# Decay attention: scores by three products of rounded high and low parts, and one buffer of turned shares

## The chip, the cores and the metric

The kernel runs on one core of one Trainium2 chip. The metric is the time of one execution on the device in microseconds (us). Shown times of a kernel are the median of several executions; a profiled execution has a time of its own.

## What is computed

Four layers (convolution mixer, forgetting attention, short convolution, convolution mixer) and then one more block work on a sequence of 512 tokens of width 1024 in float32. The change touches the second layer, the attention with forget gates. Cut to what matters:

```python
q = rms_norm(q.reshape(b, s_len, 16, 128), q_norm_g)
k = rms_norm(k.reshape(b, s_len, 16, 128), k_norm_g)
# per head and block of 128 queries
logits = einsum("bqhd,bkhd->bhqk", q_blk, k) * scale
logits = logits + c_blk[..., :, None] - c[..., None, :]
logits = where(causal, logits, -inf)
p = softmax(logits, axis=-1)
o = einsum("bhqk,bkhd->bqhd", p, v)
```

There are 16 heads of width 128; c is the running sum of the log forget gates. The layer's input projection makes q, k, v and a gate z; its output projection follows the attention.

## The kernel before, in words

Every engine has a program of its own, written out by hand in order, with waits on semaphores between them. Signals are counted; `wait_ge(signal, key)` waits for the step that `key` names. On an engine, everything behind a wait stands still until it is met.

Weights come in chunks of 1 MB, two slots. For each chunk ScalarE makes a rounded copy WH (`split_hi`, line 365), and the remainder WL comes about in one of two ways (`split_lo`, line 378): GpSimd subtracts, or, for chunks that `summed` names, ScalarE writes the negated rounded copy and GpSimd issues a DMA that adds the weights to it. The chunks of the attention's heads 1 to 15 are summed; the chunks of the values are not. A projection is three products in the rounded type fp32r (`gemm`): WH with HH, WH with HL, WL with HH, where HH and HL are the rounded activations and their remainder. One half of a chunk is 24 matmuls of 512 columns.

The attention (`layer_b_tensor` from line 1551, and the loops at lines 1703, 1782 and 1867 for VectorE, ScalarE and GpSimd) is a software pipeline over h from 0 to 17. In step h TensorE does, in this order: the query half of head h's projection; the turning (transposing) of the first two blocks of head h-2's shares; the key half of the projection; the other turns and, between them, the weighing of values with the shares of head h-2; the scores of head h-1 (`scores_tensor`, line 1498); the last weighing; after h = 3, 7 and 11 the values of the next four heads (96 matmuls); then the statistics of head h, the sums of squares of queries (`query_statistics_tensor`) and keys (`key_statistics_tensor`) over the 128 channels. The statistics take the rounded squares (SQHI) and their remainders (SQLO), two matmuls each, four `MR,onesr` records. In heads 0 and 1 the key's statistics stand inside the next head's projection instead, after its first six matmuls. Heads 0 and 15 (`WHOLE`) take the keys' squares whole, without a remainder.

ScalarE in step h: the split of the next chunk; the query's rounded square; two copies of turned shares (`copy_turned_scalar`, line 1751) into BPT; the key's rounded square; two more copies; the four exponentials of head h-1's softmax; then the logarithm and exponential of head h's variances, with a table load before each kind. For h = 16 it skips the first two copies, which VectorE does.

VectorE in step h: the shares of head h-2 (a reciprocal and four scalings); `normal_vector` (line 1634), which makes head h-1's normalized queries QN and keys KN by a Newton step, eight instructions; the copies of head h's raw queries and keys out of PSUM (`keep_vector`); the logits of head h-1; the output gate; the variances of head h.

GpSimd in step h: the causal fill for head h-1; `split_lo` for the next chunk; for h up to 14 the squares of queries and keys and their remainders (`square_low_gpsimd`, line 1839), four instructions; then the DMA that loads head h's decay rows. For h = 3, 7 and 11 the split is that of a value chunk, which GpSimd subtracts itself.

SyncE issues the loads of raw weights as slots come free.

BPT (line 1394) has two buffers of turned shares, taken in turn. The scores are four matmuls in fp32 on QN and KN, of 128, 256, 384 and 512 columns:

```python
pe.mm(logit_bank(h, i), QN[:, i * P:(i + 1) * P], KN[:, 0:(i + 1) * P], True, True)
```

A fp32 matmul leaves two records in the trace, a rounded one leaves one.

Of the kernel before, what the change touches and what calls it, by code (L numbers as in the profile page):

```python
# [7 lines left out]
ALU = mybir.AluOpType  # L8
ACT = mybir.ActivationFunctionType
F32 = mybir.dt.float32  # L10
F32R = mybir.dt.float32r

P = 128
# [136 lines left out]
def build_program(nc, x, vectors, b_f_bias, pe_k, w1_k, w2_k, pe_v, w1_v, w2_v, rel_bias, onehot, out,  # L150
# [3 lines left out]
    with ctx:  # L154
        def sb(name, cols, dt=F32):
            return ctx.enter_context(nc.sbuf_tensor(name, [P, cols], dt))
# [24 lines left out]
        HT = sb("HT", 2 * T)  # L181
        SQ = sb("SQ", 2 * T)
        DG = sb("DG", 2 * T)
        AR = sb("AR", 20960)
        banks = [ctx.enter_context(nc.psum_tensor(f"ps{i}", [P, T], F32)) for i in range(8)]

# [5 lines left out]

        def ar(o, n=T):
            return AR[:, o:o + n]

        def hs(tile, k, sl=slice(0, T)):
            return tile[:, k * T + sl.start:k * T + sl.stop]
# [1193 lines left out]
        b_t, b_ev, b_w, b_o, b_mask = (sig(n) for n in ("b_t", "b_ev", "b_w", "b_o", "b_mask"))  # L1391
        BZ = [ar(i * T) for i in range(KE)]
        BV = [ar(16 * T + i * NB * T, NB * T) for i in range(2)]
        BPT = [ar(24 * T + i * 1280, 1280) for i in range(2)]
        BP = [ar(29 * T + OFF[i], (i + 1) * P) for i in range(NB)]
        B1 = 29 * T + 1280
        RAW = [ar(B1 + i * T) for i in range(2)]
        QN, KN = ar(B1 + 2 * T), ar(B1 + 3 * T)
        CB, C_OFF = ar(B1 + 4 * T, 1280), [1152, 896, 512, 0]
        WHOLE = (0, 15)  # L1400
        NEGC = ar(B1 + 7 * T)
# [77 lines left out]
            op.then_inc(b_t, h, i)  # L1479

        def weigh_tensor(pe, h, i):
            s, g, o = h % 2, h // 4, (h % 4) * P
            if i == 0:
                if h % 4 == 2 and h < 12 or h == 0:
                    pe.wait_ge(b_vev_v, (h + 2) // 4, 3)
                else:
                    pe.wait_ge(b_o, h - 1)
                for tb in (0, 2):
                    pe.wait_ge(b_vev_a, g, tb)
                for tb in (1, 3):  # L1490
                    pe.wait_ge(b_vev_v, g, tb)
            pe.wait_ge(*turned(h, i))
            for k in range(i + 1):
                op = pe.mm(banks[3][:, i * P:(i + 1) * P], BV[g % 2][:, k * T + o:k * T + o + P],
                           BPT[s][:, OFF[i] + k * P:OFF[i] + (k + 1) * P], i == 0 and k == 0, k == i)
            op.then_inc(b_w, h, i)

        def scores_tensor(pe, h):
            pe.wait_ge(b_nrm, h, 0, 4)
            pe.wait_ge(b_nrm, h, 1, 4)  # L1500
            for i in range(NB):
                if i == 0:
                    pe.wait_ge(*((b_ttr, h - 1, 3) if h else (b_ft,)))
                elif i == 1:
                    pe.wait_ge(*((b_ttr, h - 1, 1) if h else (b_e8,)))
                elif h == 0:
                    pe.wait_ge(*((b_vev_v, 0, 3) if i == 2 else (b_negc,)))
                elif i == 2:
                    pe.wait_ge(*((b_var, h, 0) if h < 15 else (b_ttr, h, 0)))
                else:  # L1510
                    pe.wait_ge(b_ttr, h, 0 if h < 15 else 1)
                pe.mm(logit_bank(h, i), QN[:, i * P:(i + 1) * P], KN[:, 0:(i + 1) * P], True, True).then_inc(b_s, h, i)

        def logit_bank(h, i):
            return banks[((4, 5, 3, 6) if h == 0 else (4, 5, 2, 4) if h < 15 else (4, 5, 4, 5))[i]][:, 0:(i + 1) * P]
# [118 lines left out]
        def normal_vector(dve, h):  # L1634
# [13 lines left out]
            for half, (o, g) in both:  # L1648
                dve.wait_ge(b_nrm, h, half, 3)
                dve.stt(o, o, 1.5, RAW[half], ALU.add, ALU.mult).then_inc(b_nrm, h, half, 4)  # L1650

        def turned(h, i):

            return (b_sh, h, i, "turned") if h == 14 and i < 2 else (b_ev, h, i)

        def copy_turned_vector(dve, h, i):
            dve.wait_ge(b_t, h, i)
            dve.wait_ge(b_w, h - 2, 3)
            n = (i + 1) * P
            dve.copy(BPT[h % 2][:, OFF[i]:OFF[i] + n], banks[6 + i % 2][:, 0:n]).then_inc(b_sh, h, i, "turned")  # L1660

        def shares_vector(dve, h, some):
            r = small(4, "b_r", h)
# [19 lines left out]
        def layer_b_vector(dve):  # L1683
            dve.wait_ge(b_f, "gemm")
            dve.copy(FT, banks[4][:, :]).then_inc(b_ft)
            rms_vector(dve, 1, banks[6], 1)
            dve.wait_ge(b_turn)
            dve.wait_ge(b_fb)
            for tb in range(NB):
                dve.stt(BF[:, tb * 16:(tb + 1) * 16], banks[5][:, tb * 16:(tb + 1) * 16], RT[:, tb:tb + 1], FB,  # L1690
                        ALU.mult, ALU.add).then_inc(b_f8, "f", tb)
            dve.wait_ge(b_f8, "f", NB - 1)
            dve.ts(BMN, BF, 0.0, None, ALU.min).then_inc(b_f8, "min")
            dve.wait_ge(b_f8, "min")
            dve.wait_ge(b_abs, 2)
            dve.tt(LF, BMN, BAB, ALU.subtract).then_inc(b_f8, "log")
            diagonal(dve, "e8", 0, RT[:, 4:8])
            for n in range(KE):
                dve.wait_ge(b_z, n)
                dve.wait_ge(rb_made, 1)  # L1700
                dve.tt(BZ[n], banks[n % 4][:, :], RB, ALU.mult).then_inc(b_zq, n)
            values_vector(dve, 0)
            for h in range(18):
                if h >= 2:
                    shares_vector(dve, h - 2, range(1 if h == 16 else 0, NB))
                if h == 16:
                    copy_turned_vector(dve, 14, 0)
                    copy_turned_vector(dve, 14, 1)
                if 1 <= h <= 16:
                    normal_vector(dve, h - 1)  # L1710
                if h < 16:
                    keep_vector(dve, h, 0)
                if h < 16:
                    keep_vector(dve, h, 1)
                if 1 <= h <= 16:
                    logits_vector(dve, h - 1)
                if h >= 2:
                    dve.wait_ge(b_w, h - 2, 3)
                    dve.wait_ge(b_zs, h - 2)
                    dve.tt(BZ[h - 2], banks[3][:, :], BZ[h - 2], ALU.mult).then_inc(b_o, h - 2)  # L1720
                if h in (3, 7, 11):
                    values_vector(dve, (h + 1) // 4)
                if h < 16:
                    for half in range(2):
                        dve.wait_ge(b_stat, h, half)
                        if h:
                            dve.wait_ge(b_nrm, h - 1, half, 1)
                        else:
                            dve.wait_ge(b_e8)
                            dve.wait_ge(dg_spread, "e8")  # L1730
                        dve.stt(VAR[half], banks[2 + 5 * half][:, :], 1.0 / P, E8, ALU.mult, ALU.add).then_inc(
                            b_var, h, half)
                        if h == 15 and half == 0:
                            shares_vector(dve, 14, (0,))
            for k in range(5, KE, 2):
                dve.wait_ge(b_o, k)
                part_low(dve, 1, k, BZ[k])
            scaled_vector(dve, 1, 2, vec["c_norm"])
# [11 lines left out]

        def copy_turned_scalar(act, h, i):
            act.wait_ge(b_t, h, i)
            if h >= 2:
                act.wait_ge(b_w, h - 2, 3)
            n = (i + 1) * P
            act.act(BPT[h % 2][:, OFF[i]:OFF[i] + n], banks[6 + i % 2][:, 0:n], ACT.Copy).then_inc(b_ev, h, i)

        def layer_b_scalar(act):
            split_hi(act, FIRST_B + 1)
# [22 lines left out]
            for h in range(18):  # L1782
# [6 lines left out]
                if h >= 2 and h != 16:  # L1789
                    copy_turned_scalar(act, h - 2, 0)  # L1790
                    copy_turned_scalar(act, h - 2, 1)
                if h < 16:
                    act.wait_ge(b_p, h, 1)
                    if h:
                        act.wait_ge(b_stat, h - 1, 1)
                    act.act(SQS[1] if h in WHOLE else SQHI[1], banks[1][:, :], ACT.Square).then_inc(b_sq, h, 1)
# [42 lines left out]
        def square_low_gpsimd(pool, h, half):  # L1839
# [6 lines left out]
            pool.wait_ge(b_sqlo, h, half, 0)  # L1846
            pool.tt(SQLO[half], SQS[half], SQHI[half], ALU.subtract).then_inc(b_sqlo, h, half, 1)

        def layer_b_gpsimd(pool):
            pool.wait_ge(p_out, 0, 7)  # L1850
            pool.dma(FB, bass.AP(b_f_bias.tensor, 0, [[0, P], [1, 16]])).then_inc(b_fb, by=16)
# [15 lines left out]
            for h in range(16):  # L1867
                if h:
                    causal_gpsimd(pool, h - 1)
                if h in (3, 7, 11):  # L1870
                    pool.wait_ge(b_nrm, h - 1, 1, 4)
                split_lo(pool, HEAD_CHUNK[h] + 1)
                if h < 15:
                    square_low_gpsimd(pool, h, 0)
                if h < 15:
                    if h:
                        square_low_gpsimd(pool, h, 1)
                        pool.wait_ge(b_ttr, h - 1, 3)
                        forget_rows_gpsimd(pool, h)
                if h in (3, 7, 11):  # L1880
                    split_lo(pool, V_CHUNK[(h + 1) // 4] + 1)
                    split_lo(pool, V_CHUNK[(h + 1) // 4] + 2)
# [1209 lines left out]
```

## Time and profile before

| | |
|---|---|
| median of 3 runs | 2506.01 us (2505.83 to 2506.2) |
| the profiled execution | 2506.3 us |
| its span | 2504.2 us |
| TensorE busy (records of matmuls) | 2480.1 us, 99% of the span |
| VectorE, ScalarE, GpSimd busy | 57%, 52%, 60% |
| chain that ended last | TensorE 90%, VectorE 8% |

Times in the trace are counted from the span's start. The attention's heads lie between 500 and 854 us. Matmuls are pipelined: a record's length holds the time that its columns take and a tail that overlaps the next one, so what a matmul costs is the distance to the next record's start. In rows of the timeline several instructions of the same line and names are merged, "x26" gives their count, the first number is the start, the second the length; idle time before the row and what ended it stand in brackets. All matmuls have line L64, transposes L67, ScalarE's activations L70, VectorE's and GpSimd's operations on two tensors L73. The tiles of AR are not told apart by name; MR holds the rounded squares and their remainders, SQ the squares, DG the variances, HT and AR their logarithms and roots.

### The profile page before, as it was taken

To read this page: it belongs to the slowest core of one execution; us is meant where nothing else is said; L and a number is where in the kernel's file an instruction comes from. 1 tells how busy PE (TensorE), PEld (TensorE's weight loads), DVE (VectorE), ACT (ScalarE), POOL (GpSimd) and SP (SyncE) were. 2 spreads that over 40 slices of the span, in tenths; PEclk is the share of its full clock that TensorE was granted. 3 is DMA by queue.
4 is the path that set the end of the run, shared out by engine and by line. 5 is a ranking of instruction groups with operands and counts; after the bars stand their busy time and mean duration, and the time that the engine had idled before them with its cause. 6 is when DMAs were issued, how large, how long until landed. Compare 5 with 4: busy or idle time off the path is not lost.

```text
span 2504.2 us, 31059 instructions
## 1 busy us (share of the span) xinstructions
PE 2480.1 (99%) x11653; PEld 2019.6 (81%) x11653; DVE 1415.0 (57%) x2409; ACT 1293.5 (52%) x1989; POOL 1499.3 (60%) x1018
## 2 busy tenths in 40 slices
PE   8999999999999999999999999999999999999998
PEld 6888887888888788888888888878877778888887
DVE  7999863154455524444441899985598642633202
ACT  6889744276577632222232888954246562423222
POOL 5999665443453555444465799956445556645653
PEclk9999999999999999999999999999999999999999
DMA  7888722355556323223222778852422242222221
GB/s 212 193 177 188 168 102 86 105 144 151 142 141 155 108 99 102 90 95 101 98 90 99 171 183 179 192 141 84 137 91 86 85 143 101 85 101 101 90 95 68
DMA packets 72480, 311.82 MB, mean 125 GB/s; under 512 B 8107, under 2 KB 8331, under 8 KB 58892
## 3 DMA queue, kind: packets, MB, share of 16 engines
q1 hardware_dynamic: 49164, 224.07, 26.8%
q0 software_dynamic: 23168, 85.78, 17.8%
q8 instruction: 93, 1.52, 0.2%
q14 instruction: 55, 0.45, 0.1%
HBM read 303.92 MB, written 5.89 MB: 124 GB/s over the span
## 4 chain that ended last, share of the span: by engine, by line
PE 90%; DVE 8%; ACT 1%; DMA 1%; issue 1%; DVEq 0%; ACTq 0%
PE ps L64 87%; DVE ps L81 6%; PE ps L67 2%; DVE AR L81 0%; DVE ST L97 0%; DVE AR L73 0%; DMA WL<-in_weights 0%; ACT AR L70 0%; DVE AR L77 0%; DMA AR<-in_x 0%; ACT WH L70 0%; ACT L70 0%; DVE DG L73 0%; DVE SQ L73 0%; ACT WL L70 0%
## 5 line engine op out<-in xcount | busy, mean ns | idle before, releaser
L64 PE MATMUL ps<-HH,WH 128*128 128x512 f32 x3072 | 1212.4, 395 | 0.5 <-ACT WH L70 0.2
L64 PE MATMUL ps<-HL,WH 128*128 128x512 f32 x3072 | 1188.1, 389 | 0.0
L64 PE MATMUL ps<-HH,WL 128*128 128x512 f32 x3072 | 1094.3, 390 | 3.5 <-DMA WL<-in_weights 3.4
L73 POOL TENSOR_TENSOR WL<-WR,WH 128x1024 fp32r<-128x1024 f32 x273 | 677.9, 2504 | 674.8 <-ACT WH L70 659.5
L64 PEld LDWEIGHTS ps<-HH,WH 128*128 128x128 f32 x3072 | 577.1, 188 | 127.5 <-issue 4.5
L64 PEld LDWEIGHTS ps<-HH,WL 128*128 128x128 f32 x3072 | 577.2, 188 | 124.8 <-DMA WL<-in_weights 4.0
L64 PEld LDWEIGHTS ps<-HL,WH 128*128 128x128 f32 x3072 | 577.4, 188 | 116.5 <-issue 1.7
L70 ACT ACTIVATE WH<-WR 128x1024 fp32r<-128x1024 f32 (+1 forms) x404 | 409.2, 1046 | 441.0 <-PE ps L64 441.0
L81 DVE SCALAR_TENSOR_TENSOR ps<-AR,VEC,ps 128x512 f32<-128x512 f32 x652 | 449.6, 760 | 7.0 <-ACT ps L70 1.6
L73 POOL TENSOR_TENSOR AR<-AR 128x512 f32<-128x512 f32 x210 | 313.5, 1708 | 18.1 <-DVE HL L81 8.6
L70 ACT ACTIVATE AR<-ps 128x512 f32<-128x512 f32 (+3 forms) x263 | 135.3, 524 | 226.8 <-PE ps L64 140.0
L115 POOL DMA_DIRECT2D WL<-in_weights x131 | 146.0, 1115 | 137.7 <-ACT WL L70 137.7
L73 DVE TENSOR_TENSOR AR<-AR 128x512 f32<-128x512 f32 (+1 forms) x161 | 179.9, 1146 | 37.7 <-ACT AR L70 36.0
L70 ACT ACTIVATE AR<-AR,VEC 128x512 f32<-128x512 f32 x238 | 164.8, 730 | 47.8 <-DVE AR L73 31.3
L73 DVE TENSOR_TENSOR HL<-AR,HH 128x512 fp32r<-128x512 f32 x56 | 71.0, 1278 | 197.2 <-ACT HH L70 192.3
L73 DVE TENSOR_TENSOR AR<-ps,HT 128x512 f32<-128x512 f32 (+1 forms) x70 | 47.7, 687 | 234.0 <-PE ps L64 219.1
L64 PE MATMUL ps<-AR 128*128 128x128 f32 (+18 forms) x1146 | 160.0, 356 | 2.3 <-ACT AR L70 2.0
L64 PEld LDWEIGHTS ps<-AR 128*128 128x128 f32 (+5 forms) x1146 | 115.6, 174 | 44.2 <-issue 25.7
L70 ACT ACTIVATE AR<-AR 128x512 f32<-128x512 f32 (+3 forms) x72 | 40.9, 588 | 194.9 <-DVE AR L73 189.7
L73 POOL TENSOR_TENSOR AR<-AR,SQ 128x512 f32<-128x512 f32 x84 | 137.0, 1785 | 2.0
L70 ACT ACTIVATE WL<-WR 128x1024 fp32r<-128x1024 f32 x131 | 137.0, 1046 | 0.0
L73 DVE TENSOR_TENSOR AR<-AR,HT 128x512 f32<-128x512 f32 x48 | 70.2, 1463 | 98.6 <-ACT AR L70 98.1
(190 smaller groups left out, 2050.1 us busy)
## 6 DMA issues: line engine op xcount, KB each, us to landing
WR<-in_weights SPq DMA_DIRECT2D x105, 1024.0 KB, 4.8
WR<-in_weights SPq DMA_DIRECT2D x194, 512.0 KB, 4.8
WL<-in_weights POOLq DMA_DIRECT2D x131, 512.0 KB, 7.4
AR<-negc_rows POOLq DMA_DIRECT2D x16, 640.0 KB, 4.5
gate_rows<-WR SPq DMA_DIRECT2D x14, 256.0 KB, 3.3
AR<-gate_rows SPq DMA_DIRECT2D x14, 256.0 KB, 5.3
AR<-in_x SPq DMA_DIRECT2D x2, 1024.0 KB, 6.2
AR<-bias_by_distance POOLq DMA_DIRECT2D x1, 2048.0 KB, 8.6
```

The source lines that it names most:

```text
L64: return Op(None if self.e is None else self.e.matmul(o, l, r, start=first, stop=last, skip_group_check=True))
L67: return Op(None if self.e is None else self.e.transpose(o, i, identity))
L70: return Op(None if self.e is None else self.e.activation(o, i, f, **kw))
L73: return Op(None if self.e is None else self.e.tensor_tensor(o, a, b, op))
L81: return Op(None if self.e is None else self.e.scalar_tensor_tensor(o, a, s, b, op0, op1))
L115: return Op(None if self.e is None else self.e.dma_start(o, i, accum_op=ALU.add))
```

## The change

Queries and keys are split like the weights: ScalarE rounds QN and KN into QKH (the space of BPT's second buffer), and GpSimd subtracts, in place, for the low parts QKL (the same memory as QN and KN). The scores become three rounded products per block: high by high, high by low, low by high. In step h GpSimd does the two subtractions of head h-1 right after the causal fill, ahead of `split_lo`; for head 15 VectorE does them. ScalarE's two roundings stand behind the first two copies of turned shares and ahead of the key's square; in step 16, ahead of the copies of head 14's third and fourth block. BPT keeps one buffer, so a copy into it waits for the last weighing of the head before, not of the one before that.

```diff
+        AR_AT = nc.sbuf_base
         AR = sb("AR", 20960)
...
+        def at_ar(name, o, n=T):
+
+            return nc.alloc_sbuf_tensor_at(name, [P, n], F32R, offset=AR_AT + 4 * o)[:, :]
...
-        BPT = [ar(24 * T + i * 1280, 1280) for i in range(2)]
+        BPT = ar(24 * T, 1280)
+
+        QKH = [at_ar(f"QH{i}", 24 * T + 1280 + i * T) for i in range(2)]
...
         QN, KN = ar(B1 + 2 * T), ar(B1 + 3 * T)
+        QKL = [at_ar(f"QL{i}", B1 + (2 + i) * T) for i in range(2)]
...
         def scores_tensor(pe, h):
-            pe.wait_ge(b_nrm, h, 0, 4)
-            pe.wait_ge(b_nrm, h, 1, 4)
+            for half in range(2):
+                pe.wait_ge(*((b_sqlo, h, half, "normal") if h < 15 else (b_nrm, h, half, 5)))
...
-                pe.mm(logit_bank(h, i), QN[:, i * P:(i + 1) * P], KN[:, 0:(i + 1) * P], True, True).then_inc(b_s, h, i)
+                q, k, o = slice(i * P, (i + 1) * P), slice(0, (i + 1) * P), logit_bank(h, i)
+                pe.mm(o, QKH[0][:, q], QKH[1][:, k], True, False)
+                pe.mm(o, QKH[0][:, q], QKL[1][:, k], False, False)
+                pe.mm(o, QKL[0][:, q], QKH[1][:, k], False, True).then_inc(b_s, h, i)
...
+        def normal_low_vector(dve, h):
+            for half, o in enumerate((QN, KN)):
+                dve.wait_ge(b_y, h, "high", half)
+                dve.tt(QKL[half], o, QKH[half], ALU.subtract).then_inc(b_nrm, h, half, 5)
+
...
+                if h == 16:
+                    normal_low_vector(dve, 15)
...
         def copy_turned_scalar(act, h, i):
             act.wait_ge(b_t, h, i)
-            if h >= 2:
-                act.wait_ge(b_w, h - 2, 3)
+            if h:
+                act.wait_ge(b_w, h - 1, 3)
...
                     copy_turned_scalar(act, h - 2, 1)
+                if 1 <= h <= 16:
+                    for half, o in enumerate((QN, KN)):
+                        act.wait_ge(b_nrm, h - 1, half, 4)
+                        act.act(QKH[half], o, ACT.Copy).then_inc(b_y, h - 1, "high", half)
...
+        def normal_low_gpsimd(pool, h):
+            for half, o in enumerate((QN, KN)):
+                pool.wait_ge(b_y, h, "high", half)
+                pool.tt(QKL[half], o, QKH[half], ALU.subtract).then_inc(b_sqlo, h, half, "normal")
+
...
                     causal_gpsimd(pool, h - 1)
+                    normal_low_gpsimd(pool, h - 1)
```

The copies by VectorE (`copy_turned_vector`) and the weighing read the one buffer in the same way.

## Rows read from the trace of the kernel before

**Rows 1.** Windows: length, busy PE, PEld, DVE, ACT, POOL (instructions), clock, DMA.
```profile
500.00:854.00 354.00, 353.37 (x1763) 289.74 (x1762) 193.52 (x424) 239.39 (x406) 161.95 (x160) 1.00 0.57 146
690.74:708.09 17.35, 17.35 (x93) 14.36 (x92) 11.66 (x27) 13.75 (x24) 7.72 (x9) 1.00 0.64 159
```

**Rows 2.** Matmuls: head 0's scores (timeline), a run of rounded ones (chain), 62 columns (groups).
```profile
523.44 2.32 PE L64 MATMUL ps<-AR 128*128 128x128 f32 x8
...
2053.90 433.08 PE ps L64 x1909
...
L64 PE MATMUL ps<-AR 128*128 128x62 f32 x64 | 7.6, 291 | 0.3 <-ACT AR L70 0.3
```

**Rows 3.** Timeline of head 9, from its statistics before to those after.
```profile
690.74 1.17 PE L64 MATMUL ps<-MR,onesr 128*128 128x512 f32 x4
...
691.63 1.28 DVE L81 SCALAR_TENSOR_TENSOR DG<-ps,HT 128x512 f32<-128x512 f32 x2
...
693.53 0.61 ACT L70 ACTIVATE AR<-DG 128x512 f32<-128x512 f32 x1
...
695.46 0.63 ACT L70 ACTIVATE HT<-HT 128x512 f32<-128x512 f32 x1
...
698.81 0.88 POOL L115 DMA_DIRECT2D WL<-in_weights  x1 [2.45 <-ACT WL L70]
...
699.96 1.28 DVE L81 SCALAR_TENSOR_TENSOR AR<-AR 128x512 f32<-128x512 f32 x2
...
700.79 0.54 ACT L70 ACTIVATE AR<-ps 128x128 f32<-128x128 f32 x2
...
701.93 1.04 POOL L73 TENSOR_TENSOR SQ<-AR 128x512 f32<-128x512 f32 x1 [0.37 <-DVE AR L84]
...
703.05 1.28 POOL L73 TENSOR_TENSOR MR<-SQ,MR 128x512 fp32r<-128x512 f32 x1
...
705.74 1.27 POOL L73 TENSOR_TENSOR MR<-SQ,MR 128x512 fp32r<-128x512 f32 x1
...
708.09 1.17 PE L64 MATMUL ps<-MR,onesr 128*128 128x512 f32 x4
```

**Rows 4.** Timeline: a rounding on ScalarE and a low part on GpSimd, two of each.
```profile
830.54 1.14 ACT L70 ACTIVATE HH<-AR 128x512 fp32r<-128x512 f32 x2
...
833.90 2.52 POOL L73 TENSOR_TENSOR HL<-AR,HH 128x512 fp32r<-128x512 f32 x2
```

**Rows 5.** DMA issues in 698.5:700.4 and in 700.6:701.4, last number us to landing.
```profile
WL<-in_weights POOLq DMA_DIRECT2D x1, 512.0 KB, 5.7
...
WL<-in_weights POOLq DMA_DIRECT2D x1, 512.0 KB, 10.0
```

**Rows 6.** Timeline of head 1: normalization of head 0, key statistics of head 1.
```profile
520.45 1.29 DVE L81 SCALAR_TENSOR_TENSOR AR<-AR 128x512 f32<-128x512 f32 x2
...
527.60 0.70 PE L64 MATMUL ps<-MR,onesr 128*128 128x512 f32 x2
```

**Rows 7.** Timeline of head 7: low value weights, first product of the values.
```profile
645.20 4.70 POOL L73 TENSOR_TENSOR WL<-WR,WH 128x1024 fp32r<-128x1024 f32 x2 [3.76 <-DVE AR L81]
...
651.64 0.48 PE L64 MATMUL ps<-WH,HH 128*128 128x512 f32 x1
```

**Rows 8.** Timeline of step 16: weighing, copies, normalization and scores of head 15.
```profile
840.08 1.51 PE L64 MATMUL ps<-AR 128*128 128x128 f32 x10
840.14 0.96 ACT L70 ACTIVATE AR<-ps 128x384 f32<-128x384 f32 x2
...
843.91 1.28 DVE L81 SCALAR_TENSOR_TENSOR AR<-AR 128x512 f32<-128x512 f32 x2
...
845.29 3.62 PE L64 MATMUL ps<-AR 128*128 128x128 f32 x16 [0.20 <-DVE AR L81]
```

**Rows 9.** Timeline and window of TensorE's clock after an idle time, columns as in rows 1.
```profile
31.78 3.44 PE L64 MATMUL ps<-HH,WL 128*128 128x512 f32 x8 [3.44 <-DMA WL<-in_weights]
...
32.21:35.62 3.41, 3.41 (x10) 2.67 (x9) 0.26 (x1) 0.00 (x0) 0.00 (x0) 0.50 1.07 279
```

More of the change, by code:

```diff
@@ L1481, in weigh_tensor @@
         def weigh_tensor(pe, h, i):
-            s, g, o = h % 2, h // 4, (h % 4) * P
+            g, o = h // 4, (h % 4) * P
             if i == 0:
@@ L1494, in weigh_tensor @@
                 op = pe.mm(banks[3][:, i * P:(i + 1) * P], BV[g % 2][:, k * T + o:k * T + o + P],
-                           BPT[s][:, OFF[i] + k * P:OFF[i] + (k + 1) * P], i == 0 and k == 0, k == i)
+                           BPT[:, OFF[i] + k * P:OFF[i] + (k + 1) * P], i == 0 and k == 0, k == i)
             op.then_inc(b_w, h, i)
         def scores_tensor(pe, h):
-            pe.wait_ge(b_nrm, h, 0, 4)
-            pe.wait_ge(b_nrm, h, 1, 4)
+            for half in range(2):
+                pe.wait_ge(*((b_sqlo, h, half, "normal") if h < 15 else (b_nrm, h, half, 5)))
             for i in range(NB):
@@ L1657, in copy_turned_vector @@
             dve.wait_ge(b_t, h, i)
-            dve.wait_ge(b_w, h - 2, 3)
+            dve.wait_ge(b_w, h - 1, 3)
             n = (i + 1) * P
-            dve.copy(BPT[h % 2][:, OFF[i]:OFF[i] + n], banks[6 + i % 2][:, 0:n]).then_inc(b_sh, h, i, "turned")
+            dve.copy(BPT[:, OFF[i]:OFF[i] + n], banks[6 + i % 2][:, 0:n]).then_inc(b_sh, h, i, "turned")
         def shares_vector(dve, h, some):
@@ L1752, in copy_turned_scalar @@
             act.wait_ge(b_t, h, i)
-            if h >= 2:
-                act.wait_ge(b_w, h - 2, 3)
+            if h:
+                act.wait_ge(b_w, h - 1, 3)
             n = (i + 1) * P
-            act.act(BPT[h % 2][:, OFF[i]:OFF[i] + n], banks[6 + i % 2][:, 0:n], ACT.Copy).then_inc(b_ev, h, i)
+            act.act(BPT[:, OFF[i]:OFF[i] + n], banks[6 + i % 2][:, 0:n], ACT.Copy).then_inc(b_ev, h, i)
         def layer_b_scalar(act):
```

## The prediction, made before the changed kernel was run

> **What bounds it now.** I read the windows view first. From 500 to 854 us, the stretch of the sixteen heads, TensorE is busy 353.37 of 354.00 us, and in one head's period (690.74 to 708.09) all 17.35 of 17.35, while GpSimd works 7.72 [rows 1]. So TensorE sets the pace, and what it saves is time, as long as nobody makes it wait. The reader is to see in the same row that the other engines' low shares hide an order: the question is how late each of them hands over, which is in the timeline.
>
> The timeline of head 9 [rows 3] gives that order. TensorE's statistics (four matmuls, 1.17 us) end at 691.91. VectorE adds them up, ScalarE takes logarithm and exponential (a table load between), VectorE normalizes until 701.24, and GpSimd, which has issued the two transfers of low weights at 698.81 and 1.9 later, squares from 701.93 and is done at 707.01. The next statistics begin at 708.09. The loop from statistics to statistics has 1.1 us to spare, and the change lengthens it.
>
> **The scores, on TensorE.** Before, four fp32 products of 128 to 512 columns leave eight records: 2.32 us, of which the last one's tail is 0.16, so 2.16 [rows 2]. After, there are twelve rounded products. A rounded record of 512 columns takes 433.08 / 1909 = 0.227 us; 128 columns less are 0.053 less at 2.4 GHz, so 384 cost 0.174 and 256 cost 0.121. For 128 columns I take 0.112, the floor that even 62-column records keep (7.6 / 64 = 0.119 with their tails) since the weights are loaded anyway. Three of each: 3 x (0.112 + 0.121 + 0.174 + 0.227) = 1.90 us, a saving of 0.26 a head. No row shows a rounded record of 128 or 256 columns. Bounds: all 3840 columns at 2.4 GHz and nothing else, 1.60 (saving 0.56); the two short forms as slow as fp32 (0.22 and 0.43), 3.15 (loss 1.0). I take 1.90, being nearest to the records of both kinds.
>
> By the Trainium skill (FP8 and Floating Point Precision, TensorE Precision Notes) true fp32 is four passes through the array; three products would then be three quarters, 1.62 us. The row of 0.227 where 512 columns alone are 0.213 says that the weight loads keep part of it; the four heads below where it counts would give 1.1 us more.
>
> **What is added elsewhere, in a regular head.** Count from the end E of the statistics.
> 1. Key variance 0.68 (half of the pair at 691.63 [rows 3]), logarithm 0.61, table load (the gap to 695.46) 1.3, hand-overs 0.1: first exponential at E + 2.7. Before it was E + 3.55, because both variances came late; now the query's statistic runs early while the key's waits.
> 2. From that exponential ScalarE is busy without a pause until its two copies of turned shares end: 700.79 + 0.54 - 695.46 = 5.87, so E + 8.55. VectorE ends its normalization 5.78 after the exponential starts, so just before [rows 3].
> 3. New: two roundings on ScalarE. The same form (AR to fp32r, 128x512) takes 1.14 for two, 0.62 for one [rows 4]. First ready E + 9.2.
> 4. New: two subtractions on GpSimd, form as HL<-AR,HH: 2.52 for two [rows 4]. E + 11.7.
> 5. Moved behind them: GpSimd's two issues of the low weights' transfers, 0.9 each. They used to be out before the square; E + 13.5.
> 6. Both squares: 1.04 + 0.08 + 1.28 each, 4.76 together: E + 18.25. Then the key's statistic, 0.65: the next E is E + 18.9.
> TensorE alone would need 17.35 - 0.26 = 17.1. So it waits 1.8 us ahead of the key statistic, the scores' saving is lost in that wait, and a head costs 18.9 - 17.35 = 1.55 more. Heads 4 to 6, 8 to 10 and 12 to 14: 9 x 1.55 = 14.0.
>
> The new wait at the scores costs nothing here: they start at 708.09 - 2.16 - 0.9 (the last weighing's eight records) = 705.0, 13.1 after E, and the low parts are there at 11.7; head h's products behind that wait aren't touched. The causal fill stays in GpSimd's idle time before E + 9.2. The one buffer of turned shares makes ScalarE wait for the previous head's last weighing, which TensorE finished before the statistics; free. The first transfer of low weights, out at E + 11.7, lands 5.7 later [rows 5] at 17.4, needed at 18.9; free, with 1.5 to spare.
>
> **The start, heads 1 and 2.** Normalization ends at 521.74 [rows 6]; subtractions end 524.6, issues 526.4, squares 531.1. The first low weights land at 524.6 + 5.7 = 530.3, and six matmuls (1.4) stand before the key statistic: 531.7 instead of 527.60, 4.1 more. Head 2's loop was shorter by those six, 15.95, and becomes 18.9: 2.95. Together 7.0.
>
> **Heads 3, 7, 11 (values follow).** GpSimd's low value weights start at 645.20 and take 4.70; values start at 651.64 [rows 7]. They come 2.5 later for the subtractions and 0.85 earlier by step 1: done 651.55, where TensorE wants them at 651.38. Nearly level: -0.1 each, -0.3. Head 15's key statistic takes no low square, so it keeps its 0.26. Together -0.5.
>
> **The tail, head 15.** ScalarE's new roundings stand ahead of its copies of head 14's third and fourth shares, now at 840.14. They wait for VectorE's last normalization, 843.91 + 1.28 = 845.19 [rows 8], so they end at 845.8 and the first copy at 846.3. TensorE's weighing of that block (the last six records of 840.08, from 840.5) waits for it, then 0.7 and fifteen matmuls (3.4) run, and the scores begin at 850.4 instead of 845.29: 5.1. VectorE's own two subtractions (0.7 each) end by 847.2, under that. Here TensorE stands still for some 5 us. After an idle of 3.44 us this trace shows the lower of the two clock levels (0.50, 1.2 GHz) for 3.41 us [rows 9], which loses 1.7: tail 6.8. The Trainium skill has the same rule (TensorE: Matmul & The Clock Gate, Why this matters for your kernels): pauses between bursts throw the clock back; the trace agrees, 0.50 after 3.44 us.
>
> **Sum.** 14.0 + 7.0 - 0.5 + 6.8 = 27.3. The profiled execution took 2506.3 (span 2504.2 and 2.1 around it), 0.3 above the median of 2506.01. 2506.3 + 27.3 = 2533.6.
>
> **Rivals.**
> - *The covers hold* (not slower). GpSimd is idle 9.6 of 17.35 us, and the low parts hide in it. It decides if the loop of steps 1 to 6 stays under 17.1, that is if 1.8 of its 18.9 isn't there. Then 16 x 0.26 = 4.2 less: 2502.1; with the lower bound of the scores 2497. Against it: the idle time lies ahead of the normalization, not behind. Chance 0.05.
> - *The low weights come late.* A second transfer of a pair landed 10.0 after its issue [rows 5]; both now go out 0.9 apart, near the raw weights' load. If the first takes 10, head h + 1 starts at E + 21.7, and with 17.2 from there to its statistics' end two periods are 38.9: 19.45 each, 0.55 x 9 = 5 more: 2538.6. For it: three transfers share the queues. Against: SyncE's load now starts well before. Chance 0.14.
> - *The clock falls at every pause.* In regular heads 1.7 at half speed brings TensorE to 18.8, still under 18.9; in heads 3, 7, 11, 15 it is paid, 6.8: 2540.4. For it: 1.8 us pauses plus short matmuls. Against: before, nothing in this stretch fell [rows 1]. Chance 0.06.
> - *The loop is shorter than I read*, the issues (1.8) overlapping the squares: regular heads level, start about 4, tail 5: 2515. Chance 0.08.
> - That the three products cost more than fp32 (3.15) would hide in nine heads and add 1.0 in four of the rest; that is in the range.
>
> **Numbers.** The forecast's case has 0.67. Its own spread: 0.5 either way in ten loops (hand-overs, issue length, VectorE against the fill), 5; the scores' bounds -1.2 to +5; the clock 1.7. Range 2522 to 2546, which takes in the second and third rivals. A measurement of this kernel tells 0.2%, 5 us, from no change: faster 0.02, within 0.03 (the first rival, split by the scores' bound), slower 0.95.
>
> **What would show it.** In the profile after: an idle of TensorE between the query's and the key's statistics matmuls (MR,onesr), about 1.8 us in nine heads, released by GpSimd; a period of 18.9; GpSimd's chain without gaps from the subtractions to the squares; the scores near 1.9; one idle of 5 us near 860, ended by ScalarE's copy. If the first idle stands ahead of a head's first product and is ended by the transfer, the second rival is right. If there is no idle and the period is 17.1, I am wrong on the order.

## The result, and the profile after

The changed kernel takes 2536.7 us (median of 4 runs, 2536.32 to 2540.91), the kernel before 2506.11 beside it: a ratio of 1.0125, 95% interval 1.0108 to 1.0143. It is slower, as forecast, 3 us above the predicted 2533.6. The profiled execution took 2536.32, its span 2534.5 is 30.3 longer than the 2504.2 of before, and all further sums are of these two spans. Of the executions below, one of the kernel with half the dose (6439.88 us) and one of the kernel before beside it (8893.99 us) were slow and are left out of the ratios.

The page of the kernel after: busy time of TensorE, then the chain that ended last, by engine.

```profile
PE 2483.5 (98%) x11717; PEld 2028.2 (80%) x11717; DVE 1420.8 (56%) x2411; ACT 1311.7 (52%) x2021; POOL 1539.1 (61%) x1048
...
PE 81%; DVE 9%; ACT 4%; POOL 4%; issue 1%; DMA 1%; DVEq 0%; POOLq 0%; ACTq 0%
```

What TensorE waited for between 500 and 890 us after (line, releaser: total us, times, longest). Before, the same view has two waits, 0.4 and 0.2.

```profile
PE ps L64 <- POOL MR L73: 18.6, 14, 2.0
PE ps L64 <- ACT AR L70: 2.8, 1, 2.8
PE ps L64 <- issue: 1.6, 1, 1.6
PE ps L64 <- POOL HL L73: 1.5, 1, 1.5
PE ps L64 <- POOL QL L73: 1.2, 1, 1.2
PE ps L64 <- DMA WL<-in_weights: 0.5, 1, 0.5
```

The first of these is the loop of the forecast: TensorE stands before the key's statistic because GpSimd's MR is late. The windows, columns as in [rows 1], show the whole stretch of heads and one regular period:

```profile
500.00:882.00 382.00, 355.25 (x1799) 297.09 (x1797) 198.32 (x423) 255.13 (x432) 201.73 (x189) 0.99 0.51 136
610.99:630.02 19.03, 17.39 (x94) 14.74 (x95) 12.02 (x26) 14.53 (x27) 10.60 (x12) 1.00 0.57 147
```

Before, 354 us of this stretch held 353.37 of TensorE [rows 1]; after, 382 hold 355.25. The period is 19.03 instead of 17.35 (18.9 was predicted), and 1.64 of it is idle. The timeline of that period, the answer to [rows 3]:

```profile
620.87 2.53 POOL L73 TENSOR_TENSOR QL<-AR,QH 128x512 fp32r<-128x512 f32 x2 [4.68 <-ACT QH L70]
...
623.35 1.75 POOL L115 DMA_DIRECT2D WL<-in_weights  x2
...
624.52 1.65 POOL L73 TENSOR_TENSOR SQ<-AR 128x512 f32<-128x512 f32 x1
...
626.25 1.29 POOL L73 TENSOR_TENSOR MR<-SQ,MR 128x512 fp32r<-128x512 f32 x1
...
627.49 1.04 POOL L73 TENSOR_TENSOR SQ<-AR 128x512 f32<-128x512 f32 x1
...
628.61 1.26 POOL L73 TENSOR_TENSOR MR<-SQ,MR 128x512 fp32r<-128x512 f32 x1
...
630.02 0.70 PE L64 MATMUL ps<-MR,onesr 128*128 128x512 f32 x2 [1.64 <-POOL MR L73]
```

GpSimd works without a gap from 620.87 to 629.87: subtractions, issues, squares, in this order, and TensorE starts 0.15 later. The record of the two issues is 1.75 long, as forecast (1.8), but the square's record begins within it, 1.17 after its start, and takes 1.65, not 1.04; the square ends 1.07 after the issues, so together they come out as predicted. The trace doesn't tell whether the square is slowed or only shown too early.

Head 1, the answer to [rows 6], and the granted clock there (the second block, columns as in [rows 1]):

```profile
525.12 0.30 PE L64 MATMUL ps<-QH,QH 128*128 128x128 f32 x1 [1.16 <-POOL QL L73]
...
529.24 0.71 PE L64 MATMUL ps<-MR,onesr 128*128 128x512 f32 x2 [1.98 <-POOL MR L73]
...
530.45 0.77 PE L64 MATMUL ps<-HH,WH 128*128 128x512 f32 x1 [0.50 <-DMA WL<-in_weights]
...
533.15 0.91 PE L64 MATMUL ps<-MR,onesr 128*128 128x512 f32 x2
```

```profile
530.34:533.75 3.41, 3.30 (x8) 2.65 (x9) 0.33 (x1) 0.63 (x1) 1.65 (x2) 0.50 0.89 206
```

After three idles the granted clock is 0.50, the level of 1.2 GHz, for 3.41 us. The tail, the answer to [rows 8], has three idles, not one (the first, shown as "issue", ends 0.11 after a subtraction HL of GpSimd, as the second does 0.15 after one):

```profile
862.65 0.47 PE L64 MATMUL ps<-HH,WH 128*128 128x512 f32 x1 [1.59 <-issue]
866.09 0.47 PE L64 MATMUL ps<-HH,WH 128*128 128x512 f32 x1 [1.49 <-POOL HL L73]
...
870.26 1.23 ACT L70 ACTIVATE QH<-AR 128x512 fp32r<-128x512 f32 x2 [4.95 <-DVE AR L81]
...
871.39 0.96 ACT L70 ACTIVATE AR<-ps 128x384 f32<-128x384 f32 x2
...
871.92 1.65 PE L64 MATMUL ps<-AR 128*128 128x128 f32 x6 [2.77 <-ACT AR L70]
```

**The balance.** I compare the starts of each head's key statistic in the two traces. Up to head 2 they have moved by 8.64, in the nine regular heads by 16.4 more, in heads 3, 7 and 11 by 0.6, and from head 14 to the end of the attention by 6.3: 32.0. The end of the span moved by 30.3, because a stretch at the lower clock near 1373 to 1410 us, far behind the change, lasted 6.83 us before and 3.41 after. That stretch differs between the traces of this document (none with one buffer alone, 6.83 with one product), and the mean clock of the kernel before varies from 0.995 to 0.998 between its executions.

### The profile page after: what moved, and what is told of

It reads as the page before. It is cut to its first block, busy times and chain, and to the rows that moved or that the text cites. A ratio compares the mean times of both kernels' runs of the same rounds, so it can differ in the third digit from the quotient of the medians.

```text
span 2534.5 us, 31222 instructions
## 1 busy us (share of the span) xinstructions
PE 2483.5 (98%) x11717; PEld 2028.2 (80%) x11717; DVE 1420.8 (56%) x2411; ACT 1311.7 (52%) x2021; POOL 1539.1 (61%) x1048
## 4 chain that ended last, share of the span: by engine, by line
PE 81%; DVE 9%; ACT 4%; POOL 4%; issue 1%; DMA 1%; DVEq 0%; POOLq 0%; ACTq 0%
PE ps L64 79%; DVE ps L81 6%; PE ps L67 2%; POOL QL L73 1%; ACT AR L70 1%; ACT WH L70 1%; POOL MR L73 1%; ACT WL L70 1%; POOL SQ L73 1%; DVE AR L81 1%; ACT L70 1%; POOL WL L115 1%; DMA WL<-in_weights 1%; DVE AR L73 1%; DVE ST L97 0%
## 5 line engine op out<-in xcount | busy, mean ns | idle before, releaser
L73 POOL TENSOR_TENSOR AR<-AR 128x512 f32<-128x512 f32 x210 | 313.6, 1708 | 18.1 <-DVE HL L81 8.6
L64 PE MATMUL ps<-AR 128*128 128x128 f32 (+16 forms) x1018 | 127.9, 347 | 4.7 <-ACT AR L70 4.7
L64 PEld LDWEIGHTS ps<-AR 128*128 128x128 f32 (+6 forms) x1018 | 96.7, 173 | 35.0 <-issue 18.6
```

The costliest lines, as they stand in the source:

```text
L64: return Op(None if self.e is None else self.e.matmul(o, l, r, start=first, stop=last, skip_group_check=True))
L73: return Op(None if self.e is None else self.e.tensor_tensor(o, a, b, op))
```

## The experiments

My theory: GpSimd's queue from the low parts to the squares sets the period, and ScalarE's roundings the tail. Rivals: the number of products, the single buffer of turned shares, the hand-over through ScalarE, the transfers.

**The issues first.** The weights' issues go ahead of the low parts, but for heads 3, 7 and 11.

```diff
-                    normal_low_gpsimd(pool, h - 1)
-                if h in (3, 7, 11):
+                if h in (3, 7, 11):
+                    normal_low_gpsimd(pool, h - 1)
                     pool.wait_ge(b_nrm, h - 1, 1, 4)
                 split_lo(pool, HEAD_CHUNK[h] + 1)
+                if h and h not in (3, 7, 11):
+                    normal_low_gpsimd(pool, h - 1)
```

> GpSimd's two issues of low weights stand ahead of its two subtractions again, except in heads 3, 7 and 11, where the changed kernel's order is kept. Theory (GpSimd's order sets the head's period): the issues took 1.17 us between the subtractions and the squares and stretched the first square by 0.6, so a regular head's period falls from 19.0 to about 17.3 us, nearly TensorE's own pace; nine heads give 15 to 16, the start 2 to 4: about 2518 us in all. Rival (the three products cost more than they save on TensorE): no change, 2536.7. Rival (the low weights' transfers land late): they leave 4 us earlier, so it also gains, but then TensorE's waits of 1.64 us in the changed kernel should stand before a head's first product, not inside the statistics.

Measured 2518.08 (2516.39 to 2519.19), ratio to before 1.0050 (1.0035 to 1.0065), 18.6 us under the changed kernel, with the same instructions. Its GpSimd and its waits of TensorE from 500 to 890:

```profile
615.19 2.53 POOL L73 TENSOR_TENSOR QL<-AR,QH 128x512 fp32r<-128x512 f32 x2 [0.35 <-ACT QH L70]
617.68 1.03 POOL L73 TENSOR_TENSOR SQ<-AR 128x512 f32<-128x512 f32 x1
```

```profile
PE ps L64 <- POOL MR L73: 4.6, 11, 1.3
PE ps L64 <- ACT AR L70: 4.0, 1, 4.0
```

The square follows the subtraction at once and takes 1.03 again; the wait for MR falls from 18.6 to 4.6, and a period from 697.40 is 17.59. The expected 2518 is met. So 18.6 of the 30 us go with the order on GpSimd's queue, with all the added work still there. The tail's wait stays, and grows to 3.96.

**All low parts by VectorE.** `normal_low_vector(dve, h - 1)` in every step, none on GpSimd.

```diff
-                if h == 16:
-                    normal_low_vector(dve, 15)
+                if 1 <= h <= 16:
+                    normal_low_vector(dve, h - 1)
...
                     causal_gpsimd(pool, h - 1)
-                    normal_low_gpsimd(pool, h - 1)
```

> All low parts of queries and keys by VectorE, none by GpSimd; GpSimd's program is that of the kernel before. Theory: the loop over GpSimd is as before, TensorE sets the pace at 17.35 less what the products save (about 0.2 to 0.26), heads gain about 3 us in all, and what stays is the tail of head 15, 6 us: about 2509 us. Rival (the products or the one buffer or ScalarE's roundings cost the time): it stays near 2536.

Measured 2520.98 (2519.16 to 2522.45), 1.0062 (1.0047 to 1.0077): the expectation missed by 12. The regular heads did what it said (17.07 to 17.28): with the three products, the one buffer and ScalarE's roundings all in place, the period is below that of the kernel before, so none of these three sets it. Two things did not:

```profile
PE ps L64 <- DVE QL L73: 6.0, 3, 2.2
PE ps L64 <- ACT AR L70: 5.0, 1, 5.0
```

The three waits of the first line are the scores of steps 3, 7 and 11. There VectorE (first row) subtracts beside GpSimd's low value weights (second row):

```profile
556.68 5.26 DVE L73 TENSOR_TENSOR QL<-AR,QH 128x512 fp32r<-128x512 f32 x2
```

```profile
556.24 5.14 POOL L73 TENSOR_TENSOR WL<-WR,WH 128x1024 fp32r<-128x1024 f32 x2 [3.16 <-DVE AR L81]
```

Two subtractions take 5.26 where two alone take 1.28 (below), and each ends 0.55 after one of GpSimd's has ended. In those regular heads where they stand beside the squares they take 3.2 to 3.6, which is covered but for some 0.2 (see the last experiment). That is how it looks when one engine waits for the other's instruction; the kernel with VectorE first, below, tests it.

**ScalarE's roundings of head 15 later.** In step 16 they move behind both copies and behind the next weights' roundings.

```diff
-                if 1 <= h <= 16:
+                if 1 <= h <= 15:
                     for half, o in enumerate((QN, KN)):
...
                 if h == 16:
                     split_hi(act, FIRST_C - 7)
+                if h == 16:
+                    for half, o in enumerate((QN, KN)):
+                        act.wait_ge(b_nrm, h - 1, half, 4)
+                        act.act(QKH[half], o, ACT.Copy).then_inc(b_y, h - 1, "high", half)
```

> For head 15 ScalarE rounds after its copies of head 14's shares and after the split of the next weights, as the order of the kernel before had those; all else as changed. Theory: the idle of 2.8 us ahead of head 14's third weighing goes, the scores of head 15 start 1.4 us after VectorE's normalization ends: 4.5 to 5.5 us less, about 2532. Rival (the tail is bound by VectorE's late normalization anyway): under 1 us.

Measured 2538.26 (2536.20 to 2542.23), 1.0134 (1.0117 to 1.0151): nothing gained, and the expected 2532 missed by 6. The idle of 2.77 ahead of the weighing is gone, and this one has come:

```profile
876.07 0.30 PE L64 MATMUL ps<-QH,QH 128*128 128x128 f32 x1 [3.86 <-DVE QL L73]
```

```profile
870.64 5.32 DVE L73 TENSOR_TENSOR QL<-AR,QH 128x512 fp32r<-128x512 f32 x2 [0.95 <-ACT QH L70]
```

The weights' roundings let GpSimd start its WL at 870.29, and VectorE's two subtractions, 1.53 in the changed kernel, take 5.32 beside it. It is the same pair of instructions as in steps 3, 7 and 11. So the recorded rival, that VectorE bounds the tail, comes nearer in time, but through this meeting and not through a late normalization.

**One product.** Only the high parts are multiplied; the two products with low parts are left out, and all else stays.

```diff
-                pe.mm(o, QKH[0][:, q], QKH[1][:, k], True, False)
-                pe.mm(o, QKH[0][:, q], QKL[1][:, k], False, False)
-                pe.mm(o, QKL[0][:, q], QKH[1][:, k], False, True).then_inc(b_s, h, i)
+                pe.mm(o, QKH[0][:, q], QKH[1][:, k], True, True).then_inc(b_s, h, i)
```

> The scores take the product of the high parts alone; the two with a low part are left out, so the scores are rounded. All waits, roundings and subtractions stay. TensorE has 1.3 us less to do in each head. Theory: in heads bound by GpSimd's order it waits those 1.3 us longer; only heads without such a wait (15, and in part 3, 7, 11) gain: 1 to 3 us in all, about 2535. Rival (TensorE's products set the time): 16 x 1.3 = 21 us less, 2516.

Measured 2541.49 (2537.41 to 2542.77), 1.0141 (1.0126 to 1.0156). TensorE has some 1.3 us less to do in each head, and the kernel is not faster, so TensorE's products don't set the time; that rival falls. Its median is 4.8 above the changed kernel's, against an expected gain of 1 to 3, but the two intervals of the ratio overlap (1.0108 to 1.0143 there), so that it is slower is not shown. In its trace the waits are longer, and the clock falls behind them (window columns as in rows 1):

```profile
PE ps L64 <- POOL MR L73: 24.8, 18, 3.2
```

```profile
613.08:616.82 3.74, 3.74 (x10) 2.93 (x11) 2.05 (x6) 2.08 (x3) 0.39 (x1) 0.55 0.71 219
```

Between 500 and 885 us eight stretches are at 0.50, six of 3.41 and two of 6.83; the changed kernel has three of 3.41 (530, 708, 872).

**One buffer alone.** The kernel before, fp32 scores, with one buffer of turned shares.

```diff
-        BPT = [ar(24 * T + i * 1280, 1280) for i in range(2)]
+        BPT = ar(24 * T, 1280)
...
-            if h >= 2:
-                act.wait_ge(b_w, h - 2, 3)
+            if h:
+                act.wait_ge(b_w, h - 1, 3)
```

> The kernel before with one buffer of turned shares instead of two, fp32 scores kept. My theory: the copy of a head's shares then waits for the last weighing of the head before it, which TensorE finished ahead of the statistics, so nothing changes: 2506 us, periods of 17.35 in the regular heads, TensorE without idle from 500 to 854. The rival (the one buffer, not the low parts, makes the loop longer) expects part of the 30 us back here: 2515 or more, with TensorE waiting for ScalarE's copies.

Measured 2506.10 (11 runs, 2503.61 to 2507.24) against 2506.15, ratio 1.0001 (0.9992 to 1.0009). The buffer costs nothing. Its window is that of [rows 1] to 0.02:

```profile
500.00:854.00 354.00, 353.39 (x1761) 289.71 (x1761) 193.83 (x424) 239.19 (x406) 162.30 (x159) 1.00 0.56 146
```

**Half the dose.** The query's low part stays with GpSimd, the key's goes to VectorE.

```diff
         def normal_low_vector(dve, h):
-            for half, o in enumerate((QN, KN)):
+            for half, o in list(enumerate((QN, KN)))[0 if h == 15 else 1:]:
...
         def normal_low_gpsimd(pool, h):
-            for half, o in enumerate((QN, KN)):
+            for half, o in ((0, QN),):
                 pool.wait_ge(b_y, h, "high", half)
...
```

> The changed kernel with the key's low part made by VectorE in every head, the query's left to GpSimd. If GpSimd's queue from the low parts to the squares sets the period, one subtraction less (1.28 us) takes the period of a regular head from 19.03 to about 17.8 and TensorE's idle ahead of the key's statistics from 1.64 to about 0.4: nine heads x 1.25 = 11, the start 1.3, so about 2524. Since VectorE's subtraction now runs beside GpSimd's, both may be stretched, which makes the period 18.0 to 18.2 and the time up to 2528. The rival (the wait for ScalarE's roundings, or the transfers of the low weights, sets the period) expects 19.0 and 2536.

Measured 2523.79 (five of six runs 2522.02 to 2524.22), 1.0071 (1.0057 to 1.0084).

```profile
615.62 1.29 POOL L73 TENSOR_TENSOR QL<-AR,QH 128x512 fp32r<-128x512 f32 x1 [4.70 <-ACT QH L70]
616.86 1.77 POOL L115 DMA_DIRECT2D WL<-in_weights  x2
```

```profile
623.59 0.70 PE L64 MATMUL ps<-MR,onesr 128*128 128x512 f32 x2 [0.49 <-POOL MR L73]
```

One subtraction of 1.28 less, and the idle falls from 1.64 to 0.49 in this head and the period to between 17.8 and 18.1. The price per instruction holds in a second dose. ScalarE's roundings are where they were (GpSimd's subtraction starts 9.17 after E in both kernels, E being the end of the statistics), so they don't set the period. The transfers are issued 1.24 earlier here, so of them this run says nothing; what speaks against them is that in the changed kernel the idle stands ahead of the key's statistic, which reads no weights.

**VectorE first, then GpSimd.** As the kernel with all low parts by VectorE, but GpSimd's value weights wait for VectorE's subtractions, and ScalarE rounds head 15 between its copies and the next weights.

```diff
...
                 if h in (3, 7, 11):
-                    pool.wait_ge(b_nrm, h - 1, 1, 4)
+                    pool.wait_ge(b_nrm, h - 1, 1, 5)
```

> All low parts by VectorE, as in the run before; in heads 3, 7 and 11 GpSimd's subtraction of the value weights now waits until VectorE's two are done, and for head 15 ScalarE rounds after its two copies of head 14's turned shares and before the next weights' roundings. Theory of contention: VectorE's subtraction took 2.5 to 2.8 us where GpSimd subtracted 1024 columns at the same time and 0.69 where it didn't, so here all are 0.7, the idles of 1.85 to 2.19 us ahead of the scores in steps 3, 7 and 11 go, one or two half-clock stretches with them, and in the tail an idle of about 2.4 ahead of head 15's scores takes the place of the one of 5.03: 2520.98 - 6 - 2.6 - 3.4 = about 2509. The rival (VectorE is late for another reason, its own queue) keeps the three idles: 2515 or more.

Measured 2510.98 (11 runs, 2507.67 to 2512.60), 1.0018 (1.0009 to 1.0027), 2 us above the expected 2509. Step 7, VectorE and then GpSimd:

```profile
646.96 1.28 DVE L73 TENSOR_TENSOR QL<-AR,QH 128x512 fp32r<-128x512 f32 x2
```

```profile
648.32 4.71 POOL L73 TENSOR_TENSOR WL<-WR,WH 128x1024 fp32r<-128x1024 f32 x2 [6.77 <-DVE QL L73]
```

1.28 for two instead of 5.26, 4.71 instead of 5.14, and all three waits at the scores are gone: making one engine wait for the other was cheaper than letting them meet. The tail moved its stall once more, and it is 4.23 and not the 2.4 that was expected:

```profile
846.81 0.79 PE L64 MATMUL ps<-HH,WH 128*128 128x512 f32 x1 [4.23 <-ACT WH L70]
```

```profile
844.58 1.23 ACT L70 ACTIVATE QH<-AR 128x512 fp32r<-128x512 f32 x2 [3.18 <-DVE AR L81]
845.72 1.99 ACT L70 ACTIVATE WH<-WR 128x1024 fp32r<-128x1024 f32 x2
```

The roundings wait 3.18 for VectorE's normalization, and the weights' roundings behind them come too late for the next stage's products. Of the three places tried for these two roundings each gave a stall of its own.

**Head 15 in fp32.** As the last, but head 15 keeps the fp32 product, with no roundings.

```diff
+                if h == 15:
+                    pe.mm(o, QN[:, q], KN[:, k], True, True).then_inc(b_s, h, i)
+                    continue
...
```

> As the kernel with VectorE's subtractions first, but head 15's scores stay the fp32 product, so that nothing new is waited for in the tail. Expected: fifteen heads x 0.17 to 0.19 us less than the kernel before, 2.7, if nothing waits: 2503.4, and no half-clock stretch near 854. The rival, that the saving is always lost in a later wait or to the clock, gives 2506 or more.

Measured 2504.56 (11 runs, 2503.54 to 2506.53) against 2506.15, ratio 0.9994 (0.9985 to 1.0002). The tail's stall is gone, and this is the best version found; the interval takes in no change, so no gain over the kernel before is shown. What the trace shows is that the products do save time when nobody waits:

```profile
783.00:800.08 17.08, 17.08 (x97) 14.77 (x96) 13.19 (x29) 14.77 (x27) 9.30 (x9) 1.00 0.63 164
```

17.08 in such heads, 17.26 to 17.28 in others, against 17.35 before. The 0.19 between the two kinds is a wait. Here is a head of the slower kind, where VectorE's subtractions meet the squares; the second block is from a head of the faster kind.

```profile
703.56 3.25 DVE L73 TENSOR_TENSOR QL<-AR,QH 128x512 fp32r<-128x512 f32 x2
706.90 0.30 PE L64 MATMUL ps<-QH,QH 128*128 128x128 f32 x1
```

```profile
720.95 1.28 DVE L73 TENSOR_TENSOR QL<-AR,QH 128x512 fp32r<-128x512 f32 x2
721.11 2.02 POOL L73 TENSOR_TENSOR SQ<-AR 128x512 f32<-128x512 f32 x1 [0.58 <-DVE AR L84]
```

TensorE's scores start 0.10 after the second subtraction ends (706.80), and the last weighing record before them stands alone for 0.23 instead of 0.03. In the faster kind VectorE has started before GpSimd, and it is the square that is longer (2.02 instead of 1.04); the subtractions end at 722.23, 1.75 ahead of the scores.

## Why the prediction was right, point by point

- **Regular heads, 9 x 1.55 = 14.0.** Measured 16.4, 1.82 each. The mechanism is the one forecast: idle before the key's statistic, released by GpSimd, its chain gapless. The loop is 19.01 to 19.04 in four of them, against 18.9. Head 9 has 19.42, with the clock at 0.50 from 707.8 on, and head 10 has 19.14. Heads 4, 8 and 12, behind the values, have 19.26 to 19.28: there the four statistics stand together, so the early start of step 1 is missing, and the subtractions begin 9.44 after E. Else the roundings are ready 9.2 after E and the subtractions done at 11.7, both as predicted. Issues and first square come out at the predicted sum, whatever the split between them.
- **The scores, 1.90.** In step 5 they take 2.0 from 624.83 to 626.82, and with no wait the records stand 0.112, 0.118, 0.174 and 0.232 apart. So the scores save 0.16 to 0.19 and not 0.26. That TensorE's own period is still the forecast's 17.1 (17.08 with head 15 in fp32) is luck: 0.08 comes from the weighing record ahead of the scores, which stands 0.03 before its successor where it stood 0.11, a term that the forecast didn't have. The term's short forms were sized right (0.112, 0.121); the first record after fp32 work (0.142) and the first of each width (0.17 at 256) were not in it.
- **A page's figure.** My forecast weighed the four passes of true fp32 by the Trainium skill (FP8 and Floating Point Precision, TensorE Precision Notes), which gave an estimate of 1.62. The trace decides for the records' spacing, 2.0.
- **The start, 7.0.** Measured 8.64. The clock's fall at 530.34 was left out: six matmuls stand 0.427 apart instead of 0.227, 1.2 us. Another 0.36 had come before head 1.
- **Values, and head 15's own saving, -0.5.** Heads 3, 7 and 11 came out 0.13 to 0.26 later each instead of 0.1 earlier, nearly level as the two opposed terms said.
- **The tail, 6.8.** Measured 6.3, a right sum from a partly wrong split. The stall at ScalarE's copy is 2.77 and not 5.1, since TensorE itself arrived later. Two idles of 1.59 and 1.49 came ahead of it, each ending 0.11 to 0.15 after a subtraction HL of GpSimd. I had counted what waits for ScalarE in step 16 and not what stands behind the low parts in GpSimd's queue.
- **Rivals.** The late transfer: the first lands 5.4 after its issue in head 5 and is in time; only in head 1 does TensorE wait for it, 0.50. The clock at every pause: one of nine regular heads in the changed kernel, five of nine in the kernel with one product, where there are two pauses in most periods. The shorter loop: the issues' records do overlap the square's, but the square ends no earlier for it. The dearer products: 2.0, not 3.15. The covers that hold: not with this order; with VectorE's order and no roundings in the tail, yes.
- The sum was 3.0 short of the span's 30.3: start 1.6, regular heads 2.4, values 0.9, tail -0.2, and -1.7 from the clock stretch near 1400.

## What to carry to other kernels

An engine that is idle for half of a period covers new work only where the idle time lies; ask what stands behind the new instruction in its queue, DMA issues included, and who ends last after it. Moving the issues ahead of the same work gave back more than half of the loss. A wait put at a shared engine's queue doesn't vanish when it is moved: three places for two roundings gave three different stalls, and only leaving them out ended it. And before work goes from GpSimd to VectorE, see what GpSimd reads at that moment.

## What the runs showed of the hardware

**VectorE beside GpSimd.** A VectorE subtraction of 128x512 fp32 with both inputs in SBUF takes 0.68 alone, 1.53 to 1.94 beside GpSimd's squares and subtractions of 512 columns, and 2.50 to 2.83 beside its subtraction of 1024 columns; GpSimd's own of 1024 columns goes from 2.35 to 2.6 (mean of two). In the one such head above where VectorE had started first, it kept its 0.68, and GpSimd's square took 2.02 instead of 1.04. Each of VectorE's longer ones ends some 0.55 after the end of the GpSimd instruction that ran when it started, so it looks like waiting and not like sharing. The kernel that puts one behind the other shows that it is the meeting that costs. The Trainium skill (SBUF — State Buffer, Who interferes with whom) says that a VectorE instruction with two SBUF inputs contends with a GpSimd instruction that reads SBUF, and calls the lock on the ports that the two share exclusive; the traces agree, 5.26 against 1.28 for two. My expectation of 2509 for the kernel with all low parts by VectorE had left it out.

**The clock after short idles.** After an idle of 1.64 us TensorE's granted clock stayed at 1.00 in eight of nine heads of the changed kernel. In the kernel with one product, where an idle of 0.7 to 1.0 stands 2.3 ahead of the one of 1.64, it fell to 0.50 for 3.41 us in five of nine regular heads; after one such pair (1.03 and 1.64, at 710.21) it did not, and what decides was not tried. So less work on TensorE, while another engine sets the period, gained nothing there: 2541.49 against 2536.7, with intervals that overlap, and eight stretches at 0.50 instead of three.

**Issues on GpSimd.** Two DMA issues in a row are shown with 0.85 and 1.14 us, 1.75 together; the next square is shown from 1.17 after their start, takes 0.6 more than alone and ends 1.07 after them. Where the two stand 1.9 apart, in the kernel with the issues first, the work behind waits for ScalarE's rounding (0.35) and not for them.
